# Latent keys of two heads from one product, their rotated part's squares added by GpSimd, and a new order of turns for twelve projections

## The chip, the cores and the metric

The kernel runs on one core of a Trainium2 chip. Times are device microseconds (us) of one execution; the number compared is the median of several. Before the change it is 2973.7 us (3 runs, 2972.79 to 2974.1).

Engines are named as in the profile: PE is TensorE's matrix multiplication, PEld its weight load, DVE is VectorE, ACT is ScalarE, POOL is GpSimd, SP is the queue that issues the weight loads. PSUM is the memory that PE writes, in eight banks; SBUF is the working memory.

## The reference

The program is one hybrid block (gated delta rule and dilated windows), then two layers of a second block. The change lies in the multi-head latent attention of these two layers. Cut to what it computes there (x is 512 tokens of width 1024):

```
def mla_mixer(z, q_norm_g, w_uq, kv_norm_g, w_ukv, q_gain, k_gain):
    cq, ckv, k_rope = jnp.split(z, [256, 256 + 128], axis=-1)          # k_rope: 32 wide
    q = (rms_norm_2(cq, q_norm_g) @ w_uq).reshape(B, S, 8, 96)
    kv = (rms_norm_2(ckv, kv_norm_g) @ w_ukv).reshape(B, S, 8, 64 + 64)
    k_nope, v = jnp.split(kv, [64], axis=-1)
    k_rope = jnp.broadcast_to(k_rope[:, :, None, :], (B, S, 8, 32))
    k = jnp.concatenate([k_nope, k_rope], axis=-1)
    q = rms_norm_2(q, q_gain)                                          # over 96 numbers
    k = rms_norm_2(k, k_gain)
    q = concat([q[..., :64], apply_rope(q[..., 64:], cos, sin)])
    k = concat([k[..., :64], apply_rope(k[..., 64:], cos, sin)])
    ... softmax(q k^T / sqrt(96)) v, for 8 heads, no mask
```

A head's key is 64 numbers of its own and 32 rotated numbers that all heads share. Its norm is taken over the 96 together, so the sum of squares is that of the own part and that of the shared part.

## The kernel before, in words

Each engine runs its own instruction list in program order and waits on semaphores. Everything is kept with features on the partitions (128 rows) and the 512 tokens along a row. A float32 product of 128x512 appears in the trace as two MATMUL records.

The stretch of the change is the "mixer" of `layers_program`, run once per layer. Two kinds of work are interleaved there by `take_turns`, which goes through one list of names (`mix_turns`) on every engine:

- A **job** makes one projection (`jobs_pe_steps`, `jobs_act_steps`, `jobs_dve_steps`). PE multiplies the weights with the latents (L665), ACT squares the result from PSUM (L696), DVE multiplies it by the gain (L742), PE sums the squares over the rows by a product with ones (L638), ACT makes the reciprocal root by Ln and Exp (L704, L707), DVE rotates 32 rows where wanted (L752, L753, L755) and writes the result scaled (L774). The second half, from the sum on, is called finish here and is done in the turn of the job after; from job 6 on (`sums_first`) the finish of the job before comes ahead of the own product, otherwise behind it.
- A **unit** is 128 queries of one head (`attn_pe_steps` and its sisters). PE forms the scores (L860), DVE takes the row maximum (L1006), ACT the exponentials (L936), PE turns them (L872, four transpositions), ACT copies them back (L947), PE multiplies with the values (L886). In the turn of unit u, PE turns the probabilities of unit u-2, forms the scores of unit u, and multiplies the values of unit u-3; ACT copies u-2 and exponentiates u; DVE takes the maximum of u. The first unit turn does the scores of units 0 and 1.

The latent attention has 16 jobs before the change (a query job and a key job for each of 8 heads, in turns) and 32 units. A key job is 64 rows wide; the squares of the rotated key's 32 rows lie ready in rows 64 to 96 of the squares' buffer of the odd jobs, and the rotated key itself in the same rows of their gained buffer, so that one sum over 96 rows and one scaling finish it. Then come 8 jobs with long weights (24 products of 128x512 each, lines L381 to L383), and the units of two further attentions.

`mix_turns` gives 5 jobs, one unit turn (units 0 and 1), and then two unit turns and a job, twenty times. POOL has no part in it: its list (`norm_pool`) sums squares of the residual and, with `memT`, of the memory tokens; this second sum is wanted only by the norm that follows the mixer.

Of the kernel before, what the change touches and what calls it, by code (L numbers as in the profile page):

```python
# [31 lines left out]
P = 128  # L32
T = 512
# [592 lines left out]
def jobs_pe_steps(e, seen, sh, jb, at, jobs, hv=None, mixed=False, early=(), sum_banks=None, inside=()):  # L626
# [92 lines left out]
def jobs_dve_steps(e, seen, sh, jb, jobs, hv=None, at=0, count_strips=False, early=()):  # L719

    for j in range(len(jobs) + 1):
        for turn in (("finish", "begin") if j in early else ("begin", "finish")):
# [22 lines left out]
            if turn == "finish" and j > 0:  # L745
# [20 lines left out]
                e.wait_ge(jb.rstd, seen.ready(jb.rstd))  # L766
                dests = [(job["dest"][0], slice(0, job["dest"][1]))] if "dest" in job else \
# [308 lines left out]
for _name, _w in (("ffn1", KT), ("mix", KT), ("memx", KT), ("memm", KT), ("ffn2", KT), ("block", KT),  # L1076
                  ("grp", KT), ("cq", 2), ("ckv", 1), ("mlaq", 1), ("mlak", 1), ("swaq", 1), ("swak", 1),
                  ("naq", 1), ("nak", 1), ("memq", 1), ("memk", 1), ("sink", 4)):
# [22 lines left out]
def layers_program(nc, banks, xT, const, A, out, stored):  # L1101

    credit = {}
    with ExitStack() as ctx:
# [56 lines left out]
        kr_sq = sc.sem("rope_key_squared")  # L1161
        oT_done = sc.sem("oT_done")
# [34 lines left out]
        N_JOBS = 2 * MLA_HEADS + 8 + 4  # L1197
# [15 lines left out]
        def plan(layer):  # L1213
# [4 lines left out]
            for h in range(MLA_HEADS):  # L1218
# [34 lines left out]
            def units(kind):  # L1253

                out = []
                for h in range(MLA_HEADS if kind == "mla" else 4):
                    for t in range(TT):
                        tok = slice(t * P, (t + 1) * P)
                        k0, k1, bias, slot = 0, TT, None, h % 4 * TT + t
                        if kind == "mla":  # L1260
# [3 lines left out]
                            needs = [(jb.done, jobs_before + 2 * h + 2)] + (  # L1264
                                [(v_done, layer * (2 * TT + 2) + 2 * TT)] if h == 0 else [])
                        else:
# [3 lines left out]
                            needs = [(jb.done, jobs_before + 2 * MLA_HEADS + tile + 2), (padded, layer * 8 + tile + 2)]  # L1270
# [11 lines left out]
                        if kind == "mem":  # L1282
                            k1 = NMEM // P
                            v = lambda kt, h=h: v_mem[:, kt, h * DH:(h + 1) * DH]
                            needs = [(jb.done, jobs_before + 2 * MLA_HEADS + 8 + 3 + h // 2)]
# [21 lines left out]
        for name in mix_turns:  # L1307
            act_turns.append(name)
            if name == "job":
                if job in sums_first:  # L1310
                    act_turns += ["norm"] * (4 if job == 22 else 0) + ["job"]
# [6 lines left out]
        sna_at = v_at + 4 + 5 + 2 * MLA_HEADS  # L1318
# [46 lines left out]
        with nc.Block() as block:  # L1365

            @block.sync
            def _(e):
                seen = Tally(credit)
                for layer in range(LAYERS):  # L1370
# [11 lines left out]
                    with seen.loop(e, MLA_HEADS // 4, free=[(sh.strip_done, 8)]) as it:  # L1382
                        for h in range(4):
# [1841 lines left out]
```

## Time and profile before

| what | value |
|---|---|
| median of 3 runs | 2973.7 us |
| the profiled execution's own time | 2973.22 us |
| its span | 2971.4 us |
| PE busy | 2889.4 us (97%), 13458 instructions |
| PEld busy | 2315.0 us (78%) |
| DVE busy | 1452.0 us (49%) |
| ACT busy | 1087.5 us (37%) |
| POOL busy | 223.9 us (8%) |
| first product of a latent job, layers 0 and 1 | at 1169.72 and 2269.92 us |

How to read it: the span runs from the first to the last instruction, and the execution's own time is 1.8 us more. PE is the engine that is nearly always busy, so what another engine does counts where PE has to wait for it. Its clock has two levels, 2.4 GHz (1.00 in the rows) and 1.2 GHz (0.50).

### The profile page before, as it was taken

The numbers are of one execution on the slowest core, as the hardware profiler recorded it, in microseconds if no ns is written. First come the engines' busy times: TensorE is split into PE (matmuls) and PEld (weight loads), VectorE is DVE, ScalarE is ACT, GpSimd is POOL, SyncE is SP. The second block draws the span as 40 slices with busy tenths as digits, with TensorE's granted clock in tenths as the row PEclk, the third lists the DMA queues.
The fourth block names the chain that finished last, engine by engine and source line by source line (L and its number), as shares of the span: only waits on it lengthen the run. The fifth ranks groups of instructions, "written<-read, shape, count | busy, mean of one in ns | idle before, by whom it ended". The sixth has DMA issues, their size and how long they took to land.

```text
span 2971.4 us, 36175 instructions
## 1 busy us (share of the span) xinstructions
PE 2889.4 (97%) x13458; PEld 2315.0 (78%) x13458; DVE 1452.0 (49%) x2090; ACT 1087.5 (37%) x1777; POOL 223.9 (8%) x166
## 2 busy tenths in 40 slices
PE   8999999999999999998999999999999999999998
PEld 5698777788788886677788888888886677788886
DVE  5673376543444434555454443544335655454432
ACT  4512343433332223655432222332224655433221
POOL 0000000000100021000120003000121001110011
PEclk9999999999999999999999999999999999999999
DMA  3201211134222322110222232223322111132232
GB/s 118 71 22 47 78 64 57 36 92 142 79 99 92 106 89 107 36 50 29 78 85 95 95 109 89 90 94 99 105 92 86 41 50 43 64 99 92 98 108 77
DMA packets 68364, 238.08 MB, mean 80 GB/s; under 512 B 10272, under 2 KB 12448, under 8 KB 67616
## 3 DMA queue, kind: packets, MB, share of 16 engines
q1 hardware_dynamic: 66240, 227.87, 23.3%
q10 hardware_dynamic: 2016, 8.77, 0.8%
q8 instruction: 68, 1.11, 0.2%
q14 instruction: 40, 0.33, 0.0%
HBM read 234.51 MB, written 2.10 MB: 80 GB/s over the span
## 4 chain that ended last, share of the span: by engine, by line
PE 68%; DVE 3%; ACT 2%; issue 1%; DVEq 0%; ACTq 0%
PE bank L381 19%; PE bank L383 19%; PE bank L382 19%; PE bank L860 3%; PE bank L886 2%; PE bank L665 2%; PE bank L872 2%; PE bank L638 1%; ACT L_probs L936 1%; DVE L_scores L984 1%; PE bank L1518 0%; PE bank L227 0%; ACT L_h_hi L1648 0%; PE bank L1461 0%; DVE L_area L1827 0%
## 5 line engine op out<-in xcount | busy, mean ns | idle before, releaser
L381 PE MATMUL bank<-L_h_hi,L_w_hi 128*128 128x512 f32 x1776 | 703.9, 396 | 6.1 <-DVE residual L1837 3.8
L382 PE MATMUL bank<-L_h_lo,L_w_hi 128*128 128x512 f32 x1776 | 692.2, 390 | 0.0
L383 PE MATMUL bank<-L_h_hi,L_weight_ring_low 128*128 128x512 f32 x1760 | 685.9, 390 | 0.0
L369 ACT CAST L_w_hi<-L_weight_ring 128x1024 fp32r<-128x1024 f32 (+2 forms) x290 | 324.1, 1118 | 909.5 <-PE bank L383 898.6
L375 DVE TENSOR_TENSOR L_weight_ring_low<-L_weight_ring,L_w_hi 128x1024 fp32r<-128x1024 f32 (+2 forms) x290 | 393.5, 1358 | 377.9 <-ACT L_w_hi L369 377.8
L381 PEld LDWEIGHTS bank<-L_h_hi,L_w_hi 128*128 128x128 f32 x1776 | 334.1, 188 | 82.2 <-issue 5.7
L382 PEld LDWEIGHTS bank<-L_h_lo,L_w_hi 128*128 128x128 f32 x1776 | 334.3, 188 | 74.2 <-issue 5.7
L383 PEld LDWEIGHTS bank<-L_h_hi,L_weight_ring_low 128*128 128x128 f32 x1760 | 330.6, 188 | 69.8
L381 PE MATMUL bank<-L_act_hi,L_w_hi 128*128 128x512 f32 x704 | 273.9, 389 | 0.0
L382 PE MATMUL bank<-L_act_lo,L_w_hi 128*128 128x512 f32 x704 | 273.9, 389 | 0.0
L383 PE MATMUL bank<-L_act_hi,L_weight_ring_low 128*128 128x512 f32 x704 | 273.9, 389 | 0.0
L381 PE MATMUL bank<-B_h_hi,B_w_hi 128*128 128x512 f32 x480 | 200.8, 418 | 3.9 <-ACT B_arena L2688 1.8
L383 PE MATMUL bank<-B_h_hi,B_weight_ring_low 128*128 128x512 f32 x480 | 189.0, 394 | 0.0
L382 PE MATMUL bank<-h_low,B_w_hi 128*128 128x512 f32 x480 | 188.8, 393 | 0.0
L557 DVE TENSOR_TENSOR L_up<-bank,L_rstd 128x512 f32<-128x512 f32 x88 | 60.8, 691 | 245.9 <-PE bank L383 245.9
L375 DVE TENSOR_TENSOR B_weight_ring_low<-B_weight_ring,B_w_hi 128x1024 fp32r<-128x1024 f32 (+1 forms) x94 | 106.5, 1133 | 127.8 <-ACT B_w_hi L369 125.2
L886 PEld LDWEIGHTS bank<-L_area,L_probsT 128*128 128x128 f32 x960 | 131.1, 192 | 43.1 <-issue 27.9
L382 PEld LDWEIGHTS bank<-L_act_lo,L_w_hi 128*128 128x128 f32 x704 | 132.1, 188 | 27.7
L383 PEld LDWEIGHTS bank<-L_act_hi,L_weight_ring_low 128*128 128x128 f32 x704 | 132.1, 188 | 27.4
L381 PEld LDWEIGHTS bank<-L_act_hi,L_w_hi 128*128 128x128 f32 x704 | 132.1, 188 | 27.2
L369 ACT CAST B_w_hi<-B_weight_ring 128x1024 fp32r<-128x1024 f32 (+1 forms) x94 | 91.6, 974 | 151.5 <-PE bank L383 150.9
L212 POOL TENSOR_TENSOR L_squares_sum<-residual 128x512 f32<-128x512 f32 x8 | 10.0, 1252 | 1582.3 <-DVE residual L588 983.3
(338 smaller groups left out, 3874.4 us busy)
## 6 DMA issues: line engine op xcount, KB each, us to landing
L_weight_ring<-ffn_in SPq DMA_DIRECT2D x174, 512.0 KB, 3.3
L_weight_ring<-ffn_out SPq DMA_DIRECT2D x64, 704.0 KB, 4.1
B_weight_ring<-w_sqk SPq DMA_DIRECT2D x24, 512.0 KB, 3.3
B_weight_ring<-w_dn SPq DMA_DIRECT2D x16, 512.0 KB, 3.3
B_weight_ring<-w_gate SPq DMA_DIRECT2D x16, 512.0 KB, 3.3
L_weight_ring<-w_sna_qk SPq DMA_DIRECT2D x16, 512.0 KB, 3.3
L_weight_ring<-w_mix_out SPq DMA_DIRECT2D x16, 512.0 KB, 3.3
B_weight_ring<-w_sv SPq DMA_DIRECT2D x12, 512.0 KB, 3.3
```

Of the source, the lines that this page charges most:

```text
L369: e.copy(hv.high(at)[:, 0:width], hv.raw(sh, at)[:, 0:width]).then_inc(hv.w_hi_done, 1)
L375: e.tensor_tensor(hv.low(at)[:, 0:width], hv.raw(sh, at)[:, 0:width], hv.high(at)[:, 0:width].bitcast(F32), ALU.subtract).then_inc(hv.w_lo ...
L381: e.matmul(out, a_hi, b_hi, start=start, stop=False)
L382: e.matmul(out, a_hi, b_lo, start=False, stop=False)
L383: return e.matmul(out, a_lo, b_hi, start=False, stop=stop)
L557: e.tensor_tensor(hv.up[:, :], sh.banks[2 * j + 1][:, :], sh.rstd[:, :], ALU.mult)\
L638: e.matmul(banks[sum_banks[b % len(sum_banks)]][:, 0:width], ones[0:kn, :], jb.sq[0:kn, b, 0:width], start=True, stop=True).then_inc(jb.su ...
L665: mm = e.matmul(bank[r0:r0 + rn, 0:job["width"]], w[:, off:off + rn], rhs, start=(i == 0 and m == 0), stop=(i == len(job["parts"]) - 1 and ...
L860: e.matmul(banks[b][:, 0:nk], q, k, start=True, stop=True).then_inc(at_.scored, 1)
L872: mm = e.transpose(banks[b][:, i * P:(i + 1) * P], at_.p[:, u % 2, kt * P:(kt + 1) * P], ident[:, :])
L886: mm = e.matmul(banks[at_.ob[ob]][:, c0:c0 + unit["dv"]], at_.pt[:, u % 2, i * P:(i + 1) * P], v, start=(i == 0), stop=(i == len(vs) - 1))
L936: e.activation(at_.p[:, u % 2, 0:nk], src, ACT.Exp, bias=at_.nm[:, s:s + 1], accum_out=at_.sums[:, s:s + 1]).then_inc(at_.exped, 1)
```

## The change

**The jobs.** The key jobs of two heads become one: one product of 128 rows (64 of either head), one square, one gain (`mlak2`, the 64 key gains twice), and one sum with `ones64`, the matrix that has ones in two blocks of 64, which gives each head its own sum in its own 64 rows. So there are 12 latent jobs instead of 16, in the order q0, k0+k1, q1, q2, k2+k3, q3, and so on; the strips of weights fall from 16 to 12 per layer.

**The rotated key.** It is now kept apart, in rows 32 to 96 of half of the `squares` buffer (two additions of 32x512 on DVE instead of one), and its squares in the other half, once in rows 0 to 32 and once in rows 64 to 96 (two ACT squares instead of one), with zeros between from a POOL memset. Since the product fills all rows of the squares' buffer, POOL adds these squares to the job's own squares, 96 rows by 512, before PE may take the sum: a new wait of PE on `rope_added`. The finish of a key job writes four pieces: 64 own rows and 32 rotated rows for either head, each times its reciprocal root.

**The turns.** 4 jobs come first instead of 5, then 41 unit turns; a latent job stands behind unit turns 2, 4, 7, 9, 11, 15, 17 and 19 (before: 3, 5, 7 and so on). From turn 25 on the order is as before.

**POOL.** The four additions stand ahead of the memory tokens' sum.

```diff
@@ jobs_pe_steps, finish
         e.wait_ge(jb.rstd, seen.free(jb.rstd) + fewer)
+        if "sum_needs" in job:
+            e.wait_ge(*job["sum_needs"])
         e.matmul(banks[sum_banks[b % len(sum_banks)]][:, 0:width], ones[0:kn, :], jb.sq[0:kn, b, 0:width], start=True,
@@ jobs_dve_steps, finish
                 e.wait_ge(jb.rstd, seen.ready(jb.rstd))
+                if "key_pair" in job:
+                    rope_key = job["rope_key"]
+                    for half, dest in enumerate(job["key_pair"]):
+                        own = slice(half * NOPE, (half + 1) * NOPE)
+                        rope = slice(32 + half * 32, 64 + half * 32)
+                        e.tensor_tensor(dest[0:NOPE, :], jb.g[own, b, :], jb.rs[own, b, :], ALU.mult)
+                        x = e.tensor_tensor(dest[NOPE:QK2, :], rope_key[rope, :], jb.rs[rope, b, :], ALU.mult)
+                    x.then_inc(jb.done, 1)
+                    continue
@@ plan
-                mix_jobs.append(dict(parts=[[(0, ckv[:, 0, :])]],
-                                     rows=(0, NOPE), width=T, ones=(ones, QK2), scale=1.0 / QK2, gain=g("mlak"),
-                                     dest=(qk[:, tile + 1, :], QK2), split=False))
+                if h % 2 == 0:
+                    mix_jobs.append(dict(parts=[[(0, ckv[:, 0, :])]], rows=(0, P), width=T, ones=(ones64, P),
+                                         scale=1.0 / QK2, gain=g("mlak2"), split=False, rope_key=rope_key,
+                                         sum_needs=(rope_added, layer * (MLA_HEADS // 2) + h // 2 + 1),
+                                         key_pair=(qk[:, tile + 1, :], qk[:, tile + 3, :])))
@@
-                            needs = [(jb.done, jobs_before + 2 * h + 2)] + (
+                            needs = [(jb.done, jobs_before + 3 * (h // 2) + 2 + h % 2)] + (
@@ the turns
-        sums_first = range(6, 2 * MLA_HEADS + 8 + 1)
-        mix_turns = ["job"] * 5 + ["unit"]
-        for i in range(20):
-            mix_turns += ["unit"] + ["split"] * (i >= 10) + ["unit"] + {18: ["norm_used"]}.get(i, []) + ["job"]
+        sums_first = range(6, N_MLA + 8 + 1)
+        mix_turns = ["job"] * 4
+        for u in range(1, 42):
+            mix_turns += ["unit"] + ["split"] * (u >= 22 and u % 2 == 0) + ["norm_used"] * (u == 39)
+            mix_turns += ["job"] * (u in (2, 4, 7, 9, 11, 15, 17, 19) or u >= 25 and u % 2 == 1)
@@ ACT
-                    e.activation(jb.sq[NOPE:QK2, 1, :], jb.g[NOPE:QK2, 0, :], ACT.Square).then_inc(kr_sq, 1)
                     latent_rstd(2, 1, cq_rstd)
+                    for rows in (slice(0, 32), slice(NOPE, QK2)):
+                        e.activation(rope_squares[rows, :], jb.g[NOPE:QK2, 0, :], ACT.Square).then_inc(kr_sq, 1)
@@ DVE, ahead of the jobs
-                    e.tensor_tensor(jb.g[lo, 1, :], jb.g[lo, 1, :], jb.tmp[lo, :], ALU.add).then_inc(lat_done, 1)
...
+                    e.wait_ge(kr_sq, 2 * layer + 2)
+                    e.tensor_tensor(rope_key[32:64, :], jb.g[lo, 1, :], jb.tmp[lo, :], ALU.add)
+                    e.tensor_tensor(rope_key[lo, :], jb.g[lo, 1, :], jb.tmp[lo, :], ALU.add).then_inc(lat_done, 1)
@@ POOL
                     norm_pool(e, seen, sh, xT)
+                    e.wait_ge(kr_sq, 2 * layer + 2)
+                    e.memset(rope_squares[32:64, :], 0.0).then_inc(rope_zero, 1)
+                    e.wait_ge(rope_zero, layer + 1)
+                    for p in range(MLA_HEADS // 2):
+                        j = 3 * p + 1
+                        e.wait_ge(jb.squared, layer * N_JOBS + j + 1)
+                        e.tensor_tensor(jb.sq[0:QK2, j % 2, :], jb.sq[0:QK2, j % 2, :], rope_squares[0:QK2, :],
+                                        ALU.add).then_inc(rope_added, 1)
                     e.wait_ge(small, 64 * layer + 64)
                     norm_pool(e, seen, sh, memT, NMEM, wait_x=False)
```

PE, one piece of the steady pattern before the change, from the sum of job 5 to the product of job 7. L665 is a job's product (two rows for a query, one for keys), L638 a sum; L872, L860 and L886 are a unit's transpositions, scores and values:

```order
L638 MATMUL bank<-L_unsplit,shared_consts 128x512
L665 MATMUL bank<-L_area,L_weight_ring 128x512 x2
L872 MATMUL bank<-shared_consts,L_probs 128x128 x4
L860 MATMUL bank<-L_qk 128x512
L886 MATMUL bank<-L_area,L_probsT 128x64 x4
L872 MATMUL bank<-shared_consts,L_probs 128x128 x4
L860 MATMUL bank<-L_qk 128x512
L886 MATMUL bank<-L_area,L_probsT 128x64 x4
L638 MATMUL bank<-L_unsplit,shared_consts 128x512
L665 MATMUL bank<-L_area,L_weight_ring 64x512
```

The same engine in the changed kernel, from the product of job 5 (L667 is now the product, L640 the sum, L883, L871 and L897 a unit's three):

```order
L667 MATMUL bank<-L_area,L_weight_ring 128x512 x2
L640 MATMUL bank<-L_unsplit,shared_consts 128x512
L883 MATMUL bank<-shared_consts,L_probs 128x128 x4
L871 MATMUL bank<-L_qk 128x512
L897 MATMUL bank<-L_area,L_probsT 128x64 x4
L883 MATMUL bank<-shared_consts,L_probs 128x128 x4
L871 MATMUL bank<-L_qk 128x512
L897 MATMUL bank<-L_area,L_probsT 128x64 x4
L883 MATMUL bank<-shared_consts,L_probs 128x128 x4
L871 MATMUL bank<-L_qk 128x512
L897 MATMUL bank<-L_area,L_probsT 128x64 x4
L640 MATMUL bank<-L_unsplit,shared_consts 128x512
```

Behind that sum three units now follow without a job between them, where two did.

DVE in the same piece before the change: the maxima of two units, the one scaling that finishes a key job (L774), the gain of a query job, the next two maxima, and the first instruction of a query's rotation:

```order
L1006 TENSOR_REDUCE L_neg_max<-bank 128x1 x2
L774 TENSOR_TENSOR L_qk<-L_gained,L_job_rstd 96x512
L742 TENSOR_SCALAR L_gained<-bank,L_scaled_q_gains 128x512
L1006 TENSOR_REDUCE L_neg_max<-bank 128x1 x2
L752 TENSOR_TENSOR L_up<-L_gained,L_rope_cos_sin 32x512
```

And in the changed kernel, at job 5 (L744 is the gain, L774 and L775 the four pieces of two keys, L1017 the maximum):

```order
L1017 TENSOR_REDUCE L_neg_max<-bank 128x1 x2
L744 TENSOR_SCALAR L_gained<-bank,L_scaled_q_gains 128x512
L774 TENSOR_TENSOR L_qk<-L_gained,L_job_rstd 64x512
L775 TENSOR_TENSOR L_qk<-L_squares,L_job_rstd 32x512
L774 TENSOR_TENSOR L_qk<-L_gained,L_job_rstd 64x512
L775 TENSOR_TENSOR L_qk<-L_squares,L_job_rstd 32x512
L1017 TENSOR_REDUCE L_neg_max<-bank 128x1 x3
```

The one scaling of a key job has become four in a row, all of which need the reciprocal root, and the next unit's maximum stands behind them.

POOL in the changed kernel, around the new instructions (L217 and L219 are the square and the addition of `norm_pool`; before, the row of L212 follows directly on the first two):

```order
L217 TENSOR_TENSOR L_tile_squares<-residual 128x512
L219 TENSOR_TENSOR L_squares_sum<-L_squares_sum,L_tile_squares 128x512
L1917 MEMSET L_squares 32x512
L1922 TENSOR_TENSOR L_unsplit<-L_unsplit,L_squares 96x512 x4
L212 TENSOR_TENSOR L_squares_sum<-L_memT 128x256
L217 TENSOR_TENSOR L_tile_squares<-L_memT 128x256
```

The memory tokens' 15 instructions now wait for the fourth addition, that is for job 10.

## Rows read from the trace of the kernel before

**Rows 1.** The page's chain that ended last, by engine
```profile
PE 68%; DVE 3%; ACT 2%; issue 1%; DVEq 0%; ACTq 0%
```

**Rows 2.** Windows: length, busy PE, PEld, DVE, ACT, POOL; PEclk, DMA share, GB/s
```profile
1185.00:1190.00 5.00, 5.00 (x19) 3.32 (x20) 1.18 (x2) 2.43 (x6) 0.00 (x0) 0.66 0.01 3
...
1190.00:1260.00 70.00, 70.00 (x346) 43.20 (x345) 41.94 (x66) 45.51 (x96) 0.00 (x0) 1.00 0.11 32
...
2285.00:2290.00 5.00, 4.82 (x23) 2.94 (x24) 1.38 (x2) 3.54 (x11) 0.00 (x0) 1.00 0.00 0
```

**Rows 3.** Timeline of PE, a key step, a query step, a unit: start, us, instruction
```profile
1243.18 1.08 PE L638 MATMUL bank<-L_unsplit,shared_consts 96*128 96x512 f32 x2
...
1245.19 0.66 PE L872 MATMUL bank<-shared_consts,L_probs 128*128 128x128 f32 x4
...
1249.53 1.08 PE L638 MATMUL bank<-L_unsplit,shared_consts 96*128 96x512 f32 x2
1250.44 1.88 PE L665 MATMUL bank<-L_area,L_weight_ring 128*128 128x512 f32 x4
1252.16 0.60 PE L872 MATMUL bank<-shared_consts,L_probs 128*128 128x128 f32 x4
1252.60 1.02 PE L860 MATMUL bank<-L_qk 96*128 96x512 f32 x2
...
1254.30 0.61 PE L872 MATMUL bank<-shared_consts,L_probs 128*128 128x128 f32 x4
```

**Rows 4.** Timeline of ACT and DVE beside that query step, which finishes a key
```profile
1250.65 0.60 ACT L704 ACTIVATE L_job_rstd<-bank 128x512 f32<-128x512 f32 x1 [0.25 <-PE bank L638]
1252.86 0.58 ACT L947 COPY L_probsT<-bank 128x512 f32<-128x512 f32 x1
1254.45 0.69 ACT L936 ACTIVATE L_probs<-bank,L_neg_max 128x512 f32<-128x512 f32 x1 [1.01 <-DVE L_neg_max L1006]
1255.13 1.03 ACT L369 CAST L_w_hi<-L_weight_ring 128x1024 fp32r<-128x1024 f32 x1
...
1252.01 0.69 DVE L774 TENSOR_TENSOR L_qk<-L_gained,L_job_rstd 96x512 f32<-96x512 f32 x1 [2.42 <-ACT L_job_rstd L707]
...
1253.73 0.68 DVE L1006 TENSOR_REDUCE L_neg_max<-bank 128x1 f32<-128x512 f32 x1
```

**Rows 5.** Timeline of the stage's start, layer 0: from DVE's first gain
```profile
1172.41 0.75 DVE L742 TENSOR_SCALAR L_gained<-bank,L_scaled_q_gains 128x512 f32<-128x512 f32 x1 [3.21 <-ACT L_unsplit L696]
...
1174.18 0.69 DVE L752 TENSOR_TENSOR L_up<-L_gained,L_rope_cos_sin 32x512 f32<-32x512 f32 x1
...
1174.90 0.68 DVE L753 TENSOR_TENSOR L_gained<-L_gained,L_rope_cos_sin 32x512 f32<-32x512 f32 x1
...
1183.43 1.28 DVE L1006 TENSOR_REDUCE L_neg_max<-bank 128x1 f32<-128x512 f32 x2
1184.15 0.69 ACT L936 ACTIVATE L_probs<-bank,L_neg_max 128x512 f32<-128x512 f32 x1 [1.43 <-DVE L_neg_max L1006]
...
1184.98 0.91 PE L872 MATMUL bank<-shared_consts,L_probs 128*128 128x128 f32 x4 [1.84 <-ACT L_probs L936]
```

**Rows 6.** Timelines of DVE and POOL at layer 1's memory sum, and one residual addition
```profile
2238.28 1.22 DVE L375 TENSOR_TENSOR L_weight_ring_low<-L_weight_ring,L_w_hi 128x1024 fp32r<-128x1024 f32 x1 [5.69 <-ACT L_w_hi L369]
...
2240.45 1.28 DVE L1758 TENSOR_TENSOR L_gained<-bank,L_rstd 128x512 f32<-128x512 f32 x2
2241.95 1.81 DVE L375 TENSOR_TENSOR L_weight_ring_low<-L_weight_ring,L_w_hi 128x1024 fp32r<-128x1024 f32 x1 [0.22 <-ACT L_w_hi L369]
...
2240.68 0.61 POOL L212 TENSOR_TENSOR L_squares_sum<-L_memT 128x256 f32<-128x256 f32 x1 [14.29 <-DMA L_na_bias<-na_bias]
...
2241.94 0.73 POOL L219 TENSOR_TENSOR L_squares_sum<-L_squares_sum,L_tile_squares 128x256 f32<-128x256 f32 x1
...
2252.08 0.74 POOL L219 TENSOR_TENSOR L_squares_sum<-L_squares_sum,L_tile_squares 128x256 f32<-128x256 f32 x1
...
1403.31 1.28 POOL L219 TENSOR_TENSOR L_squares_sum<-L_squares_sum,L_tile_squares 128x512 f32<-128x512 f32 x1
```

More of the change, by code:

```diff
@@ L1161, in layers_program @@
         kr_sq = sc.sem("rope_key_squared")
+        rope_added = sc.sem("rope_squares_added")
+        rope_zero = sc.sem("rope_squares_zero")
         oT_done = sc.sem("oT_done")
@@ L1269, in units @@
                             k = qk[:, tile + 1, :]
-                            needs = [(jb.done, jobs_before + 2 * MLA_HEADS + tile + 2), (padded, layer * 8 + tile + 2)]
+                            needs = [(jb.done, jobs_before + N_MLA + tile + 2), (padded, layer * 8 + tile + 2)]
                         if kind in ("swa", "na"):
@@ L1310, in layers_program @@
                 if job in sums_first:
-                    act_turns += ["norm"] * (4 if job == 22 else 0) + ["job"]
+                    act_turns += ["norm"] * (4 if job == N_MLA + 6 else 0) + ["job"]
                 job += 1
@@ L1381, in _ @@
                     at = load_strip(e, seen, sh, at, A["w_mla_v"][layer])
-                    with seen.loop(e, MLA_HEADS // 4, free=[(sh.strip_done, 8)]) as it:
-                        for h in range(4):
-                            load_strip(e, seen, sh, at + 2 * h, A["w_mla_q"][layer, it * 4 + h])
-                            load_strip(e, seen, sh, at + 2 * h + 1, A["w_mla_k"][layer, it * 4 + h])
-                    at += 2 * MLA_HEADS
+                    for h in range(MLA_HEADS):
+                        at = load_strip(e, seen, sh, at, A["w_mla_q"][layer, h])
+                        if h % 2 == 0:
+                            at = load_strip(e, seen, sh, at, A["w_mla_k"][layer, h // 2])
                     assert at == at0 + sna_at
@@ L1657, in _ @@
                     norms, rows = group_norms(), rows_act()
-                    take_turns(act_turns, job=jobs_act_steps(e, seen, sh, jb, mix_jobs, hv, at0 + sna_at - 2 * MLA_HEADS, sums_first,
+                    take_turns(act_turns, job=jobs_act_steps(e, seen, sh, jb, mix_jobs, hv, at0 + sna_at - N_MLA, sums_first,
                                                               pause=True),
@@ L1773, in _ @@
                     seen.ready(sh.strip_done)
-                    e.wait_ge(kr_sq, layer + 1)
+                    e.wait_ge(lat_scaled, 4 * layer + 4)
                     e.wait_ge(small, 64 * layer + 64)
@@ L1787, in _ @@
                                                in1=cq_rstd, op0=ALU.mult, op1=ALU.mult).then_inc(lat_done, 1)
+                    e.wait_ge(kr_sq, 2 * layer + 2)
+                    e.tensor_tensor(rope_key[32:64, :], jb.g[lo, 1, :], jb.tmp[lo, :], ALU.add)
+                    e.tensor_tensor(rope_key[lo, :], jb.g[lo, 1, :], jb.tmp[lo, :], ALU.add).then_inc(lat_done, 1)
+                    e.wait_ge(lat_done, 4 * layer + 4)
                     def scale_groups():
@@ L1817, in _ @@
                     scales, rows = scale_groups(), rows_dve()
-                    take_turns(mix_turns, job=jobs_dve_steps(e, seen, sh, jb, mix_jobs, hv, at0 + sna_at - 2 * MLA_HEADS, True, sums_first),
+                    take_turns(mix_turns, job=jobs_dve_steps(e, seen, sh, jb, mix_jobs, hv, at0 + sna_at - N_MLA, True, sums_first),
                                unit=attn_dve_steps(e, seen, sh, at_, mix_units, stores("mix", o_tok, 8)),
@@ L3104, in layout2 @@
         two(a["swa_q_gain_2"]), two(a["swa_k_gain_2"]), two(a["na_q_gain_2"]), two(a["na_k_gain_2"]),
-        two(a["mem_q_gain_2"]), two(a["mem_k_gain_2"]),
+        two(a["mem_q_gain_2"]), two(a["mem_k_gain_2"]), two(a["mla_k_gain_2"][:, :64]),
         np.broadcast_to(a["swa_sink_2"][:, None, :], (L, P, 4))], -1)
```

16 lines of the change are left out of this document (9 added, 7 removed).

## The prediction, made before the changed kernel was run

> **What bounds the kernel now.** I read the chain of waits first: 68% of it is PE, and DVE and ACT have 3% and 2% [rows 1]. So time is won where PE has less to do, and lost where it has to wait. Then I read the windows of the stage that the change touches. From 1190 to 1260 us PE is busy for 70.00 of 70.00 us, while DVE has 41.94 and ACT 45.51 [rows 2]: work that PE is spared there shows in full, as long as the others keep up. Ahead of it lies the start of the stage. DVE takes its first gain at 1172.41 and its first maximum only at 1183.43, after it has worked through five jobs, and PE then waits 1.84 us for the first exponential and starts the first transposition at 1184.98 [rows 5]. There DVE's list, not PE, sets the time.
>
> Last I read how the clock answers to a wait. The 5 us after that wait have a granted clock of 0.66, so a part of them ran at 1.2 instead of 2.4 GHz; in the second layer the same stretch after the same wait has 1.00 [rows 2]. 5 us times 0.34 is 1.7 us, the price of one fall.
>
> **What PE is spared.** In the steady pattern a step that multiplies a key and takes a sum lasts from 1243.18 to 1245.19, 2.01 us; the step of a query from 1249.53 to 1252.16, 2.63 us, of which the sum is 0.91 and the two products 0.86 each [rows 3]. The trace has no key product of 128 rows. Its bounds are the query's 0.86 and what the 64-row key takes now, 2.01 less the sum, 1.10; I take 0.86, since the query's product has the same shape. A step with a key pair is then 1.77. After the first transposition there were six key steps in a layer and will be three: 3 x 2.01 and 3 x 0.24, together 6.75 us less per layer (6.0 with the upper bound). What is spared ahead of the first transposition is worth nothing, since DVE sets that time.
>
> **The start.** From the first gain to the first maximum DVE has 11.02 us [rows 5]: five gains of 0.75 and ten instructions with both inputs in SBUF (two rotations of three, four scalings), which follow each other every 0.72 (1174.18, 1174.90). In the new order it has four gains and twelve such (two rotations, two scalings of queries, four pieces of a key pair): that is 2 x 0.72 - 0.75 = 0.7 us more.
>
> To it comes POOL. In the memory tokens' sum a split on DVE, whose two inputs lie in SBUF, takes 1.81 instead of 1.22 us when it begins beside a POOL addition of 0.73; two DVE instructions that read PSUM keep their 1.28 and POOL its 0.61 [rows 6]. So two-input SBUF work on DVE waits until POOL's instruction is through, and gains and maxima, which read PSUM, don't. POOL's addition of 96x512 isn't in the trace; 0.73 (256 columns) and 1.28 us (128x512) bound it [rows 6], and I take 1.28, of the nearer width. It begins with DVE's gain of the key pair (0.75), so the rotation behind the gain starts 0.5 us late. The start is 1.2 us later per layer, between 0.7 and 1.2. PE's new wait for the addition costs nothing itself: it ends while PE is busy with q1's product (1.72).
>
> The rest ahead of the jobs I take as nothing: the two ACT squares and the second DVE addition lie in the idle 3.21 us before the first gain [rows 5], SP has four short loads fewer and no queue in front of them, and the memset comes before any job. At worst they move the first product by one instruction, 0.7.
>
> **The stalls.** Here the four pieces in a row matter, since the maxima of the next units are queued behind them. On the way of a unit, its maximum begins 0.72 before its exponential and that 0.83 before its transposition [rows 5]: 1.55 us. PE's unit is 2.14 (1252.16 to 1254.30) [rows 3].
>
> *Behind turn 4.* Count from the first transposition. PE: unit 2, key pair, sum 3.1; units 3 and 4 7.4; product of q3 9.1, sum 10.05, units 5 and 6, so that unit 5 is to be turned at 14.35. The others: the key pair's square ends at 3.8; DVE's gain to 4.65, but the addition on POOL lasts to 5.2, then rotation and scaling of q2, 4 x 0.72, to 8.05; maximum of unit 3, exponential at 8.75 (0.83), copy 0.58, exponential of unit 4 to 11.0, ACT's square for q3 0.60 [rows 4], then the roots of the key pair from 11.6. From the start of Ln to the piece that waits for it are 1.36 (1250.65 to 1252.01) [rows 4], so the pieces run from 13.0 to 15.8, the maximum of unit 5 stands behind them, and the transposition can start at 17.35. PE waits 3.0 us.
>
> *Behind turn 11.* Sum first: the first piece comes 2.48 after it (1249.53 to 1252.01) [rows 3, 4], four pieces 2.88, the gain 0.7, then the maximum at 6.05 and its transposition at 7.6. PE gets there after sum, product and two units, 0.91 + 1.72 + 4.28 = 6.9, and no job stands between: 0.7 us.
>
> *Behind turn 19.* The same 0.7, and the memory tokens' sum. It lasts 12.1 us (2240.68 to 2252.82) [rows 6] and stood ahead of the jobs; now it follows the addition for job 10, some 4.4 us after the sum in turn 17, and the four pieces begin 8.5 after that sum, in its middle. Each waits for the POOL instruction in progress, 0.6 as the split did: 2.4 more, 3.1 in all.
>
> *Behind the split of turn 22.* ACT's half is 1.03 [rows 4], DVE's 1.22 [rows 6]; from unit 22's start, maximum 1.5, exponential 2.2 to 3.05, the halves to 5.5, the next maximum and its 1.55: 7.05, against three units of PE, 6.4. 0.6 us, since the job that followed is gone.
>
> Together 7.4 us per layer, and none is under other work, since PE's own list is in order. If DVE and ACT catch up faster than I count, it is nothing.
>
> Of the Trainium skill one rule is weighed here. The rows show the blocking for instructions of 128 rows only, and the pieces have 64 and 32. SBUF — State Buffer, section "Who interferes with whom", says that an instruction with two SBUF inputs contends with a GpSimd instruction that reads SBUF and that the later one is held for the other's full length, whatever the shape. By the rule my 0.5, 0.55 (of the 3.0) and 2.4 stand; if small pieces passed, the sum would be 3.45 less per layer.
>
> **The sum.** Per layer -6.75 + 1.2 + 7.4 = +1.85, in both 3.7. The clock: six waits of about 3 us arise (start, turn 4, turn 19, in two layers) where two of 1.84 stood and one brought a fall. I take four falls against one, 3 x 1.7 = 5.1; the bounds are none more and five more, 0 and 8.5. Forecast 8.8 us slower on the profiled execution's 2973.2 (span 2971.4 and 1.8 around it), 2982.0; that execution lies 0.5 below the median of the three runs, 2973.7.
>
> **The rivals.**
> - *The lists keep up (faster).* PE never waited from 1190 to 1260 with DVE at 60% [rows 2], and if the four pieces fit in as well, only the start remains: 2 x (0.7 - 6.75) = -12.1, 2961. For it: ACT loses four squares and four pairs of roots per layer. Against: the order of the queues, not the load, makes my stalls, and the new turns put two or more units without a job behind the key pairs.
> - *POOL does not hold the small pieces (the same).* Then 3.45 less per layer, -3.2 in both, and with one fall more of the clock 2972. It decides at the rows of the pieces: 0.7 us each or 1.3.
> - *The clock falls after every wait (slower still).* Five falls more, 3.7 + 8.5 = 12.2, 2985.5. Against it: one of two equal waits brought none.
>
> **Chances.** Forecast 0.40, faster rival 0.26, the same 0.24, the clock 0.10. The range of 8 in 10 goes from 2961, the faster rival, to 2990, the clock's case with the start's extra 0.7 and the upper bound of the key product (1.5 in both layers) and some more; the forecast's own range is 2975 to 2988. Within 0.2% (6 us, about what a measurement of this kernel can tell from no change) I put the POOL rival and a little of the forecast's low end, 0.27; faster 0.25, slower 0.48.
>
> **What will show it.** In the profile after: steps with a key pair at 1.77 on PE; the first transposition some 16.4 us behind the first product instead of 15.3; a wait of PE ahead of the transposition in the third unit behind q3's product, of 3 us; the four pieces behind turn 19 spread over 5 us with POOL instructions between them, and PE waiting about 3 us two units later; a clock below 1.00 behind some of these. I am wrong if PE stays fully busy from the first transposition to the long jobs, or if the four pieces follow each other every 0.72 beside POOL's memory sum.

## The result, and the profile after

The changed kernel takes 2986.44 us (median of 5 runs, 2972.76 to 2991.06) against 2973.46 (5 runs, 2972.47 to 2974.1) for the kernel before, measured alongside: ratio 1.0038, 95% interval 1.0024 to 1.0052, so 13.0 us slower. Measured a second time (e1) it was 2988.37 against 2971.78 (ratio 1.0060, 1.0046 to 1.0073), 16.6 slower. The forecast was 2982.0, 8.8 slower. The first five runs of the changed kernel differ by 18 us, and their time follows their mean granted clock: 2972.8 us at 0.986, 2991.1 at 0.980. The kernel before has 0.988 to 0.990 in the 24 runs beside e1.

The profiled execution took 2983.65 us (span 2981.6, before 2971.4). The page's chain that ended last, against [rows 1]:

```profile
PE 65%; DVE 5%; ACT 2%; issue 2%; DMA 0%; DVEq 0%; ACTq 0%
```

PE has 3 points less in that chain, DVE 2 more and issue 1 more. Its waits in the stage of layer 0 stand in the timeline of PE; the number in brackets is the idle time ahead of the row, and L883 is a unit's transposition:

```profile
1179.62 2.73 PE L871 MATMUL bank<-L_qk 96*128 96x512 f32 x4 [2.14 <-DVE L_qk L775]
1184.69 1.12 PE L883 MATMUL bank<-shared_consts,L_probs 128*128 128x128 f32 x4 [2.34 <-ACT L_probs L947]
...
1203.69 0.65 PE L883 MATMUL bank<-shared_consts,L_probs 128*128 128x128 f32 x4 [1.49 <-ACT L_probs L947]
...
1229.70 0.66 PE L883 MATMUL bank<-shared_consts,L_probs 128*128 128x128 f32 x4 [0.42 <-ACT L_probs L947]
...
1255.91 1.12 PE L883 MATMUL bank<-shared_consts,L_probs 128*128 128x128 f32 x4 [1.83 <-ACT L_probs L947]
```

They are the start's two, and those behind turns 4, 11 and 19. The prediction named all these places but the first: the wait of 2.14 us stands ahead of the first scores, which need the last of the four pieces (L775) of the first key pair. Before, the work that PE had ahead of these scores filled the time. Layer 1 waits at the same five places (2.14, 3.09, 1.48, 0.42, 1.83). Before there was one wait of 1.84 and one of 0.44 in the stage of either layer.

Windows of the same stage (columns as in [rows 2]) show the clock behind them:

```profile
1178.00:1192.00 14.00, 10.03 (x20) 4.45 (x21) 8.89 (x14) 5.16 (x12) 1.27 (x1) 0.63 0.04 11
1192.00:1202.00 10.00, 10.00 (x57) 6.92 (x55) 6.50 (x10) 4.93 (x11) 0.00 (x0) 1.00 0.05 13
1202.00:1214.00 12.00, 10.51 (x36) 6.27 (x36) 6.05 (x10) 5.49 (x12) 0.00 (x0) 0.72 0.02 5
1214.00:1254.00 40.00, 39.58 (x210) 26.65 (x209) 27.21 (x43) 23.87 (x51) 11.08 (x13) 1.00 0.18 57
1254.00:1264.00 10.00, 8.17 (x34) 6.04 (x34) 4.25 (x6) 5.21 (x11) 2.84 (x5) 0.66 0.00 0
```

The clock is 1.00 except around and behind the start's two waits and behind those of 1.49 and 1.83 us. A stretch in which the granted clock is at its lower level is called a fall here. Read in windows of 2 us, PE's clock was at 1.2 GHz for 10.2, 6.8 and 6.8 us in layer 0, and for 6.8 in layer 1; before it was 3.4 in all. The stage, from the first latent product to the first long product, lasts 99.79 and 92.12 us in the two layers, before 93.58 and 91.90: 6.4 us more. The other 3.8 of the 10.2 by which the spans differ lie outside both stages (2789.7 against 2785.9). The profiles of e1, e5, e6, e7 and e11 have 2783 to 2785 there, e1 being the changed kernel itself, so I take that part for scatter.

The start (DVE and POOL, against [rows 5]):

```profile
1171.26 0.75 DVE L744 TENSOR_SCALAR L_gained<-bank,L_scaled_q_gains 128x512 f32<-128x512 f32 x1 [2.75 <-ACT L_unsplit L698]
1172.09 0.75 DVE L744 TENSOR_SCALAR L_gained<-bank,L_gains 128x512 f32<-128x512 f32 x1
1172.87 1.07 DVE L754 TENSOR_TENSOR L_up<-L_gained,L_rope_cos_sin 32x512 f32<-32x512 f32 x1
1173.98 0.68 DVE L755 TENSOR_TENSOR L_gained<-L_gained,L_rope_cos_sin 32x512 f32<-32x512 f32 x1
...
1183.15 1.28 DVE L1017 TENSOR_REDUCE L_neg_max<-bank 128x1 f32<-128x512 f32 x2
...
1172.12 1.27 POOL L1922 TENSOR_TENSOR L_unsplit<-L_unsplit,L_squares 96x512 f32<-96x512 f32 x1 [4.67 <-ACT L_unsplit L698]
```

POOL's addition takes 1.27 us, and the rotation (L754) that begins beside it 1.07 instead of 0.69. The four pieces behind turn 19, inside POOL's memory sum (against [rows 4, 6]):

```profile
1249.48 1.01 DVE L774 TENSOR_TENSOR L_qk<-L_gained,L_job_rstd 64x512 f32<-64x512 f32 x1 [1.52 <-ACT L_job_rstd L709]
1250.50 1.01 DVE L775 TENSOR_TENSOR L_qk<-L_squares,L_job_rstd 32x512 f32<-32x512 f32 x1
1251.52 1.12 DVE L774 TENSOR_TENSOR L_qk<-L_gained,L_job_rstd 64x512 f32<-64x512 f32 x1
1252.66 1.01 DVE L775 TENSOR_TENSOR L_qk<-L_squares,L_job_rstd 32x512 f32<-32x512 f32 x1
...
1249.22 0.72 POOL L219 TENSOR_TENSOR L_squares_sum<-L_squares_sum,L_tile_squares 128x256 f32<-128x256 f32 x1
1249.90 1.06 POOL L217 TENSOR_TENSOR L_tile_squares<-L_memT 128x256 f32<-128x256 f32 x1
1251.04 1.06 POOL L219 TENSOR_TENSOR L_squares_sum<-L_squares_sum,L_tile_squares 128x256 f32<-128x256 f32 x1
```

Both engines are slowed: DVE's pieces from 0.68 to 1.01 and 1.12, POOL's square (L217) from 0.61 and its addition (L219) from 0.72 to 1.06.

### The profile page after: what moved, and what is told of

Read it like the earlier page. It is cut to its first block, busy times and chain, and to the rows that moved or that the text cites. A ratio compares the mean times of both kernels' runs of the same rounds, so it can differ in the third digit from the quotient of the medians.

```text
span 2981.6 us, 35953 instructions
## 1 busy us (share of the span) xinstructions
PE 2884.9 (97%) x13426; PEld 2319.5 (78%) x13426; DVE 1461.6 (49%) x2100; ACT 1075.6 (36%) x1755; POOL 234.2 (8%) x176
## 4 chain that ended last, share of the span: by engine, by line
PE 65%; DVE 5%; ACT 2%; issue 2%; DMA 0%; DVEq 0%; ACTq 0%
PE bank L381 19%; PE bank L382 19%; PE bank L383 19%; PE bank L871 2%; PE bank L897 2%; PE bank L883 1%; PE bank L640 1%; PE bank L667 1%; ACT L_probs L947 1%; DVE L_scores L995 0%; PE bank L1535 0%; DVE L_qk L774 0%; DVE L_qk L775 0%; DMA L_weight_ring<-w_latent 0%; DVE L_neg_max L1017 0%
## 5 line engine op out<-in xcount | busy, mean ns | idle before, releaser
L897 PEld LDWEIGHTS bank<-L_area,L_probsT 128*128 128x128 f32 x960 | 133.7, 196 | 44.7 <-issue 29.3
L897 PE MATMUL bank<-L_area,L_probsT 128*128 128x64 f32 x960 | 128.7, 271 | 0.9 <-ACT L_probsT L958 0.8
```

The source lines that it names most:

```text
L897: mm = e.matmul(banks[at_.ob[ob]][:, c0:c0 + unit["dv"]], at_.pt[:, u % 2, i * P:(i + 1) * P], v, start=(i == 0), stop=(i == len(vs) - 1))
```

## The experiments

The first theory was that the waits cause the loss, each by its own length and more so by the clock behind it. Its rivals were that the clock falls anyway in this stage, or that something else of the change (the extra work of DVE and POOL) costs the time. The experiments ran in three sets on three chips: e1 to e4 beside the kernel before at 2971.78 us, e5 to e8 at 2972.08, e9 to e11 at 2972.46. A time that is compared across sets carries this difference. "Mean clock" is that of a kernel's runs, "ratio" is to the kernel before with its 95% interval, and "theory A" and "theory B" are those of the expectation just above.

**e1, the changed kernel again.** No edit.

> The changed kernel once more, as the reference of this set. The clock theory (PE's new waits make the granted clock fall, now in one run, now in another) expects a wide spread again, some 2971 to 2991 us, and a median between 2980 and 2988; the instruction order and the lengths of DVE's and ACT's work as in the first profile, and a difference between the runs that goes with their mean clock, 3 us for each 0.001. The rival, a fixed loss by the queues alone, expects a spread of 2 us as the kernel before has.

2988.37 us (5 runs, 2986.43 to 2991.62), mean clock 0.981. The median is just above the range that I gave, and the wide spread didn't come again: 5.2 us, where the kernel before has 6.7 in 24 runs. So the spread decides nothing here; the loss and the lower clock are what came again. The waits behind the three turns are the same to 0.01 us; the second of the start's is shorter where PE reaches it at the lower clock (2.27 and 1.37 us). What differs is how long the clock stays low. Windows of the two stages, and of the 22 us behind turn 19's wait:

```profile
1167.64:1272.72 105.08, 96.91 (x397) 60.89 (x397) 63.58 (x93) 55.26 (x115) 16.46 (x19) 0.83 0.09 30
2281.31:2377.62 96.31, 88.97 (x397) 55.09 (x397) 60.54 (x89) 53.95 (x113) 16.47 (x19) 0.91 0.10 33
...
1254.00:1276.00 22.00, 21.00 (x66) 15.33 (x67) 8.73 (x13) 10.49 (x21) 2.00 (x3) 0.53 0.00 1
```

The clock was at 1.2 GHz for 54.6 us in five falls (the one behind turn 19 ends 3 us after its stage), in the first profile for 30.6 in four. Behind turn 19 alone it stayed low for 20 us.

**e2, POOL's memory sum ahead of the four additions.**

```
+  e.wait_ge(small, 64 * layer + 64)
+  norm_pool(e, seen, sh, memT, NMEM, wait_x=False)
   e.wait_ge(kr_sq, 2 * layer + 2)
+  e.wait_ge(sh.sq_summed, 5 * layer + 3)
   e.memset(rope_squares[32:64, :], 0.0).then_inc(rope_zero, 1)
...
-  e.wait_ge(small, 64 * layer + 64)
-  norm_pool(e, seen, sh, memT, NMEM, wait_x=False)
```

> The changed kernel with the memory tokens' sum on POOL back ahead of the four additions. The theory that POOL holds DVE's four pieces behind turn 19 expects these pieces every 0.70 us instead of every 1.03, PE's wait behind turn 19 at 0.4 instead of 1.83 us (as the 0.42 behind turn 11), and one fall of the clock less per layer where one came there: 2.8 us for the waits in two layers and 2 to 6 with the clock, so a median of 2978 to 2984. The rival that POOL's order is of no account (DVE's order alone) expects the wait unchanged and the median within 2 us of the changed kernel's.

The added wait makes POOL begin the memset only when its sums are done; the four additions follow in the part left out. 2975.26 us (11 runs; ratio to before 1.0009, 1.0000 to 1.0018), mean clock 0.9845: 13.1 below e1, and below the 2978 to 2984 expected. DVE, and PE two units later:

```profile
1250.77 0.68 DVE L774 TENSOR_TENSOR L_qk<-L_gained,L_job_rstd 64x512 f32<-64x512 f32 x1 [1.52 <-ACT L_job_rstd L709]
1251.47 0.68 DVE L775 TENSOR_TENSOR L_qk<-L_squares,L_job_rstd 32x512 f32<-32x512 f32 x1
...
1255.79 0.66 PE L883 MATMUL bank<-shared_consts,L_probs 128*128 128x128 f32 x4 [0.42 <-ACT L_probs L947]
```

The pieces follow each other every 0.70 again and the wait falls from 1.83 to 0.42. So the memory sum makes 1.41 of it, 2.8 us in both layers together. The other 10 of the 13.1 are more than the waits' length; no fall stands behind turn 19 any more, where e1's profile had one of 20 us. The four falls at the start and behind turn 4 are still there.

**e3, the jobs spread evenly.**

```
-  mix_turns += ["job"] * (u in (2, 4, 7, 9, 11, 15, 17, 19) or ...
+  mix_turns += ["job"] * (u in (3, 5, 7, 9, 11, 13, 15, 17) or ...
```

> The changed kernel with the latent jobs behind unit turns 3, 5, 7 to 17, at even spacing, in place of 2, 4, 7, 9, 11, 15, 17, 19. The theory that DVE's four pieces hurt where no job follows within two units expects no wait of PE behind the second job after the start (before 1.49 us) and none behind turn 11 (0.42); behind the last one the wait stays, since eight units follow it. 3.8 us less in two layers, and falls of the clock that came behind these waits gone: a median of 2974 to 2982. The rival that the four pieces cost the same wherever they stand expects the waits moved, not gone, and the median unchanged.

2968.74 us (11 runs, 2964.33 to 2983.23; ratio to before 0.9997, 0.9985 to 1.0008), mean clock 0.985: 19.6 below e1, and below the 2974 to 2982 expected. The waits behind turns 4 and 11 (1.83 at full clock and 0.42) are gone; the start's two and the one behind the last key pair (1.84 and 1.83) remain. That is 4.5 us of length in both layers, and leaves 15 for the clock. The one fall of 20 us in its profile stands behind the wait of 1.84.

**e4, dummy products in the start's waits.** 2 products of 128x512 ahead of the first scores and 3 ahead of the first transposition, overwritten afterwards.

```
+    def fill(u, i):
+        for _ in range(units[u]["fill"][1][i]):
+            e.matmul(banks[at_.tb[0]][:, :], sh.ones[:, :], units[u]["fill"][0], start=True, stop=True)
...
+            mix_units[0]["fill"] = (cs2[:, :], (2, 3))
```

> The changed kernel with five products of 128x512 that nothing reads on PE in the two waits of the start (two ahead of the first scores, three ahead of the first transposition), which would otherwise be idle. The clock theory expects that the first transposition stays where it is, within 0.3 us, that the clock no longer falls there (in the profile 3.4 us and more at half in either layer), and so 2 to 3 us less per layer, a median of 2978 to 2983. The rival that the fall there costs nothing because DVE's list sets the time expects no difference; if the products come late they cost up to 0.5 us per layer.

2980.30 us (8 runs; ratio to before 1.0030, 1.0019 to 1.0040), mean clock 0.985: 8.1 below e1, where I had expected 4 to 6 (the median lies in the range given), though the first transposition comes no earlier (16.16 behind the first product, as in e1). The start no longer brings a fall. Behind the waits at turns 4 and 19, 1.83 each in both layers, the clock falls in three cases of four.

**e5, all waits over 1 us filled.** As e4, and 2 dummy products ahead of the transpositions of units 5 and 20.

```
+            for u in (5, 20):
+                mix_units[u]["fill"] = (cs2[:, :], (0, 2))
```

> The changed kernel, with dummy products of 128x512 (0.86 us each, their result is overwritten) put into the waits of PE: 2 ahead of the first scores and 3 ahead of the first transposition, as in e4, and now also 2 ahead of the transposition behind turn 4 (unit 5) and 2 ahead of the one behind turn 19 (unit 20), where 1.83 us of waiting are left at full clock. No real instruction moves: stage length at full clock stays 82.9 plus about 7.7 us of waits and dummies. Theory A, the waits cost mostly through the clock (bookkeeping: the changed kernel has 7 to 8 us less of full-clock work and waits than before, and loses 20 us by a mean clock of 0.981 against 0.989): with PE busy in the waits the mean clock returns to about 0.988 and the time to 2968 (2965 to 2973), some 12 below e4's 2980.3. Theory B, the waits cost their own length and the clock's falls come from elsewhere in the stage: no more than e4, 2980 (2977 to 2983).

2968.09 us (12 runs; ratio to before 0.9984, 0.9975 to 0.9993), mean clock 0.990. Windows of its stages:

```profile
1167.51:1258.22 90.71, 89.15 (x414) 54.84 (x415) 60.55 (x89) 53.47 (x113) 16.45 (x19) 1.00 0.11 35
2265.44:2356.15 90.71, 89.15 (x414) 54.84 (x415) 60.55 (x89) 53.48 (x113) 16.45 (x19) 1.00 0.11 35
```

Both are 90.71 us long at a clock of 1.00, against 91.90 in the layer of before that has no fall. The real instructions come no earlier than the waits would let them; only the falls are gone, and with that the change is a small gain: theory A. The rival that the clock falls anyway is out, and so is the one that the extra work of DVE and POOL costs more than these waits. Of the 4.0 us to the kernel before, some 2.4 are this gain (1.19 in either layer) and the rest, some 1.7, is the fall that the kernel before has in layer 0.

**e6, e2 and e3 together.**

> The changed kernel with both edits of e2 and e3: jobs behind turns 3, 5, 7 ... 17, and POOL's memory sum ahead of the four additions. Theory A: the waits behind turns 4 and 11 are gone (as in e3), the one behind the last key pair shrinks from 1.83 to 0.42 (as in e2), and only the start's two waits (2.15 and 2.3 to 3.1) are left. Against e3's 2968.7 that is 2 x 1.41 = 2.8 less by its own length and some 5 less by the clock: 2961 (2957 to 2965), faster than both kernels. Theory B, the gains of e2 and e3 are the same gain (the clock falls once per stage whatever waits are left): 2966 to 2969.

2964.76 us (11 runs; ratio to before 0.9980, 0.9972 to 0.9989), mean clock 0.986. Faster than both kernels. Only the start's two waits are left, with a fall of 10.2 us behind them in either layer:

```profile
1166.71:1256.37 89.66, 84.80 (x397) 53.53 (x397) 58.96 (x89) 53.35 (x113) 5.24 (x4) 0.94 0.11 35
2263.16:2352.47 89.31, 85.21 (x397) 53.40 (x397) 58.99 (x89) 53.36 (x113) 5.25 (x4) 0.94 0.11 35
```

That is inside theory A's range (2957 to 2965), but at its very end and 1.2 below theory B's (2966 to 2969): against e3 the time fell by 4.0, of which 2.8 is the wait's length, so the clock gave some 1 and not 5. The two gains add up in part only.

**e7, e6 with the start's dummy products.**

> e6 with 2 dummy products ahead of the first scores and 3 ahead of the first transposition, in both layers. No real instruction moves (first transposition 16.16 us behind the first product). Theory A: the clock no longer falls at the start; in e4 this was worth 8 us, here the same or a little less: e6 less 6 to 8, about 2954. Theory B, the start's fall is only put off to the next small wait: the same as e6 within 2 us.

2960.77 us (5 runs, 2958.47 to 2962.76; ratio to before 0.9964, 0.9952 to 0.9977), mean clock 0.990. It is the fastest of all, 11.3 us below the kernel before. 4.0 below e6 lies between the theories (6 to 8, and under 2); the two profiles differ by 5.6 in their stages.

```profile
1166.84:1253.52 86.68, 85.24 (x406) 53.49 (x407) 58.98 (x89) 53.35 (x113) 5.25 (x4) 1.00 0.12 36
2260.20:2346.89 86.69, 85.25 (x407) 53.51 (x407) 58.98 (x89) 53.36 (x113) 5.25 (x4) 1.00 0.11 36
```

86.7 us at full clock against 91.90 is 5.2 per layer, 10.4 in both: nearly all of the 11.3.

**e8, waits without the change.** The kernel before, with eight further maxima on DVE ahead of that of units 6 and 20; nothing reads them.

```
+        for i in unit.get("again", ()):
+            e.tensor_reduce(at_.nm[:, i:i + 1], src, AX.X, ALU.max, negate=True)
...
+            for u, i in ((6, 16), (20, 24)):
+                mix_units[u]["again"] = range(i, i + 8)
```

> The kernel before the change, with DVE taking eight further maxima of the same scores (0.62 us each, 5.0 together, into unused columns) ahead of the maximum of units 6 and 20 of the latent attention, in both layers. The exponentials have about 3.1 us of slack there, so PE should wait 1.8 to 2 us at two places per layer, as the changed kernel does behind turns 4 and 19; nothing else of the change is in it. Own length: 2 x 2 x 1.9 = 7.6 us. Theory A, such waits bring falls of the clock (half speed for some 7 us each, 3.4 us lost): 4 of them cost up to 13 us more, so 2971.8 + 7.6 + 8 to 13 = 2987 to 2993, mean clock 0.984 to 0.986. Theory B, the waits cost only their length: 2979 (2977 to 2982), clock 0.989 as before.

2979.87 us (10 runs; ratio 1.0025, 1.0015 to 1.0034), mean clock 0.990: theory B. PE waits 1.60, 1.58, 1.60 and 1.59, 6.4 us together, of 7.8 measured. My theory A was wrong as it stood: behind these four waits there is one fall, of 3.4 us.

**e9, longer waits without the change.** As e8, with ten further maxima.

> As e8, but with ten further maxima ahead of the same two units instead of eight: in e8 PE waited 1.60 and 1.58 us there at a mean clock of 0.990, so two more maxima of 0.62 us make it 2.8 us at each of four places, 4 x 2.8 = 11.3 us against the kernel before, 4.9 more than e8. Theory A, the length of a wait decides whether the clock falls (1.6 us is too short, 2.8 is not): 2979.9 + 4.9 + up to 4 x 3.4 = 2990 to 2998, mean clock 0.985 to 0.987. Theory B, it is two waits in close succession (as at the start of the changed kernel's stage, 2.14 and 2.34 us within 6 us) that bring the fall, and a single one in full work does not: 2985 (2983 to 2987), clock 0.989 to 0.990.

3000.96 us (4 runs, 2996.34 to 3004.78; ratio 1.0091, 1.0076 to 1.0107), mean clock 0.983. Two more maxima of 0.62 in four places cost some 21 us (28.5 above the kernel before, where e8 had 7.8). The wait at unit 6 in e8 (first) and in e9, with the 13 us behind it:

```profile
1204.22 0.66 PE L872 MATMUL bank<-shared_consts,L_probs 128*128 128x128 f32 x4 [1.60 <-ACT L_probs L936]
...
1204.00:1217.00 13.00, 12.78 (x66) 8.28 (x66) 8.62 (x15) 9.85 (x24) 0.00 (x0) 1.00 0.04 12
```
```profile
1205.33 0.66 PE L872 MATMUL bank<-shared_consts,L_probs 128*128 128x128 f32 x4 [2.80 <-ACT L_probs L936]
...
1205.00:1218.00 13.00, 12.67 (x39) 8.16 (x40) 5.43 (x9) 7.26 (x18) 0.00 (x0) 0.61 0.00 1
```

All four places of e9 show 0.61 over 13 us, that is 10.2 us at half speed, 5.1 lost each and 20.4 in all; with the waits' own 11.2 this is 31.6. The profiled execution, the slowest of the four, took 32.3 more than the kernel before; the median is 28.5 more. So a longer wait is enough by itself (theory A), and no second wait near by is needed. That isn't the whole of it, though: in the changed kernel, e1 and e2 the wait behind turn 4, 1.48 or 1.49 us, begins 11 to 13 us behind the end of the start's fall, and there it brought a fall in five cases of six. The time came still higher than theory A's 2990 to 2998, since I had counted 3.4 us lost per fall.

**e10, without the first three additions.** e7, with the rotated key's squares left out of the norm of six heads.

```
-                    for p in range(MLA_HEADS // 2):
+                    for p in (3,):
```

> e7 without POOL's additions for the first three key pairs, so the rotated key's squares are left out of these six heads' norms; the fourth stays. DVE and PE keep every instruction. Theory A, POOL's addition holds DVE's first rotation behind the pair's gain (1.07 us in the changed kernel instead of 0.69): the first transposition comes 15.8 us behind the first product instead of 16.16, and what remains over the 15.26 of before, 0.5, is DVE's longer list. Theory B, the addition costs nothing there and the whole 0.9 is the list: 16.16. The time is not to be told from e7's.

One run, 2957.89 us, which is not told from e7's. The start in DVE and PE (L895 is the transposition):

```profile
1173.86 0.69 DVE L754 TENSOR_TENSOR L_up<-L_gained,L_rope_cos_sin 32x512 f32<-32x512 f32 x1
1174.57 0.68 DVE L755 TENSOR_TENSOR L_gained<-L_gained,L_rope_cos_sin 32x512 f32<-32x512 f32 x1
...
1185.29 0.66 PE L895 MATMUL bank<-shared_consts,L_probs 128*128 128x128 f32 x4 [0.51 <-ACT L_probs L959]
```

The first transposition comes 15.77 behind the first product (at 1169.52) instead of 16.16: POOL's addition costs 0.39 there, and DVE's longer list the 0.51 that remain over the 15.26 of before. Theory A.

**e11, the kernel before with dummy products.** 2 ahead of its first transposition.

> The kernel before the change with 2 dummy products (0.86 us each) in the wait of 1.84 us ahead of the first transposition, in both layers; nothing real moves. Theory A: this wait lies 6 us behind one of 0.44 and brings a fall in one layer of two (half speed for 3.4 us, 1.7 lost): 2970.4, 1 to 3 below the kernel before, so e7's lead of 11 us is hardly the dummies' alone. Theory B: filling a wait is worth as much there as in e4 (8 us): 2964.

2969.70 us (11 runs; ratio 0.9993, 0.9984 to 1.0002), mean clock 0.990. Its stages are 91.90 and 91.91 at clock 1.00. Theory A: filling is worth some 2.8 us there by the medians (none to 4.8 by the interval), so 8 or 9 of e7's 11.3 are the change, with better turns and the memory sum first.

## Why the prediction was right, and where its terms were off

The direction and the range were right (2986.4 in 2961 to 2990), and so was the mechanism: waits of PE at the places named, and falls of the clock behind some of them. But the two parts of the sum were off in opposite directions. The prediction had a loss of 3.7 us from work and waits and one of 5.1 from the clock; the runs show a gain of some 2.4 from the first (e5) and a loss of 15 to 19 from the second. That the total came within 5 us of the forecast is luck, and the change is slower for one of the two reasons only, the clock.

- **PE spared, 6.75 per layer.** Right. The pair step is 1.78 (a sum and a product, 0.92 and 0.86):

```profile
1216.15 1.08 PE L640 MATMUL bank<-L_unsplit,shared_consts 96*128 96x512 f32 x2
1217.07 1.02 PE L667 MATMUL bank<-L_area,L_weight_ring 128*128 128x512 f32 x2
1217.93 0.60 PE L883 MATMUL bank<-shared_consts,L_probs 128*128 128x128 f32 x4
```

  In e7, behind the first transposition, 86.68 - 16.16 less a wait of 0.43 is 70.1 of work, where the kernel before had 91.90 - 15.26 = 76.6: 6.5 spared.
- **The start, +1.2.** Measured 0.9: 0.5 for DVE's list (0.7 forecast) and 0.4 for POOL (0.5), told apart by e10. What the prediction left out is that PE, with one job less ahead of the first scores, now idles there as well (2.14), so that the start has two waits within 6 us, with a fall behind them.
- **The wait behind turn 4, 3.0.** Measured 1.83 at full clock (e4). The mechanism is right (e3). PE reaches the place as forecast (14.4 behind the first transposition in e4), but the roots of the key pair begin at 10.5 and not 11.6, and the pieces at 11.9 and not 13.0: my count of ACT's and DVE's instructions ahead of them was 1.1 us too long. The rows of e4, whose first transposition starts at 1182.92 (ACT, DVE, PE):

```profile
1193.44 0.61 ACT L706 ACTIVATE L_job_rstd<-bank 128x512 f32<-128x512 f32 x1
1194.82 0.68 DVE L774 TENSOR_TENSOR L_qk<-L_gained,L_job_rstd 64x512 f32<-64x512 f32 x1 [0.39 <-ACT L_job_rstd L709]
1199.18 1.07 PE L891 MATMUL bank<-shared_consts,L_probs 128*128 128x128 f32 x4 [1.83 <-ACT L_probs L955]
```

- **Behind turn 11, 0.7.** Measured 0.42.
- **Behind turn 19, 3.1.** Measured 1.83, of which 0.42 stay without the memory sum and 1.41 come with it (e2), for 0.7 and 2.4. The rival that small pieces pass POOL's instructions is out; but a piece was held for 0.33 us (one of the four for 0.44), not for 0.6. The Trainium skill (SBUF — State Buffer, section "Who interferes with whom") calls the port pair that VectorE and GpSimd share an exclusive lock, and says of VectorE's 2-port modes that the engine that issues first has it for the whole instruction; the prediction took the whole length for instructions with two SBUF inputs too. The trace agrees that pieces of 64 and 32 rows are held, and does not show the full length for alternating instructions (0.33 beside 0.61 and 0.72).
- **Behind turn 22's split, 0.6.** One gap of 0.24 there, ahead of the transposition three units later.

  The waits and the start together come to 5.2 per layer (0.9 and 4.3) where I had 8.6, so this part of the sum is -1.3 per layer and not +1.85. Taken alone it makes a faster kernel, and e5, with 1.19 less in either layer, shows one.
- **The clock, 5.1.** This is the step that was mis-sized most. I took 5 us at a clock of 0.66, 1.7 us lost, as the price of one fall, from the only fall that [rows 2] shows, which was 3.4 us long. The changed kernel's falls lasted 6.8 to 20 us. Against before, e1 loses 16.6 in spite of 2.4 of gain, so the clock took some 19 (15 in the first measurement). The profiles say the same: e1's two stages are together 20.0 longer than e5's, which have the same waits and no fall. The number of falls, four for one, was right in the first profile (e1 has five).
- **The rival that the clock falls after every wait** (2985.5; its own terms give 2985.4) came nearest in time, but not for its reason: not every wait brought a fall, each fall was longer.

What stays open: why the wait of 1.83 behind turn 19 brings a fall in layer 0 and none in layer 1 of one execution, why one fall lasts 6.8 us and another 20 behind the same wait, and what makes the shorter wait behind turn 4 enough. I found nothing in the profiles that tells the cases apart. It was not tried to shorten DVE's list at the start itself, which the dummy products only cover.

## What to carry to other kernels

A wait of the engine that bounds a kernel is not worth its own length: 1.2 us more of waiting at four places cost 21 us (e8 to e9), because the clock fell behind each. When a change takes work from PE and hands it to the lists of other engines, look for every wait of PE of 1.5 us and more that it makes, and spread what makes it: here four instructions in a row ahead of a maximum, and POOL's sum in the middle of them. Only then count the work spared. Where a wait can't be moved, dummy products in it kept the clock up at no cost in time (e4, e5, e7), but they gain only where a fall stood (e11).

## What the runs showed of the hardware

- Single waits of PE in steady work, by the profiles: at 1.6 us one fall (3.4 us at half speed) behind four waits (e8); at 1.83 or 1.84 us, behind turn 19 in the changed kernel, e1, e3 and e4 and behind turn 4 in e4, six falls behind ten; at 2.8 us four behind four, each 10.2 us long (e9). Falls of 3.4, 6.8, 10.2, 17 and 20 us at 1.2 GHz were seen.
- The start's two waits, 2.14 us and then 1.3 to 3.1, brought a fall in all ten layers that have them (changed kernel, e1, e2, e3, e6), nine of 10.2 us and one of 6.8. The start's wait of 1.84 in the kernel before, e8 and e9 brought one of 3.4 us in four layers of six.
- The changed kernel's executions took from 2972.8 to 2991.1 us in the first set, at a mean clock from 0.986 to 0.980: about 3 us for 0.001.
- DVE instructions with two SBUF inputs and POOL instructions that alternate with them slow each other: DVE from 0.68 to 1.01 (one 1.12), POOL from 0.61 and 0.72 to 1.06. Beside one POOL instruction of 1.27 us that began 0.75 earlier, DVE's took 1.07.
